# Sixteen modulation tiles moved from the second output layer to the last down layer of a two-block transformer kernel

## What is computed

```python
def second_block(x, c, w_mod, b_mod, ...):
    c_act = jax.nn.silu(c)
    mod = (c_act @ w_mod[l] + b_mod[l])[:, None, :]
    sh_m, sc_m, g_m, sh_f, sc_f, g_f = jnp.split(mod, 6, axis=-1)
    h = rmsnorm(x, mix_pre_w[l]) * (1 + sc_m) + sh_m
    y = hybrid_mixer(h, w_in[l], conv_w[l], ..., w_out[l])
    x = x + g_m * rmsnorm(y, mix_post_w[l])
    h = rmsnorm(x, ffn_pre_w[l]) * (1 + sc_f) + sh_f
    y = conv_ffn(h, w_up[l], ffn_conv_w[l], w_down[l])
    x = x + g_f * rmsnorm(y, ffn_post_w[l])
    return x
```

## Time and profile before

| | us |
|---|---|
| runs, median of 3 | 2451.34 (2451.24 to 2452.98) |
| the profiled execution's own time | 2453.18 |
| its span in the profile | 2451.3 |
| PE busy | 2429.1 (99%) |
| DVE busy | 1781.8 (73%) |
| ACT busy | 1158.0 (47%) |
| POOL busy | 124.0 (5%) |

### The profile page before, as it was taken

The page is one execution under the profiler, slowest core; times in us unless marked ns, Lnnn a source line. Parts: engine busy times, 40 slices in busy tenths (PEclk is TensorE's granted clock), DMA queues, the critical chain, the costliest instruction groups (busy, mean ns, idle before and its releaser), DMA issues.

```text
span 2451.3 us, 35393 instructions
## 1 busy us (share of the span) xinstructions
PE 2429.1 (99%) x13044; PEld 2096.0 (86%) x13044; DVE 1781.8 (73%) x2380; ACT 1158.0 (47%) x1292; POOL 124.0 (5%) x230
## 2 busy tenths in 40 slices
PE   9999999999999999999999999999999999999998
PEld 8888888888888888888888888887888888888887
DVE  5778777699898898677656677777776777775444
ACT  6454445444444444444445445455544444444443
POOL 0000000001000000011002000000000000000000
PEclk9999999999999999999999999999999999999999
DMA  7778775688888888899864655576666666666665
GB/s 256 248 251 264 224 232 187 196 271 288 280 275 293 279 280 276 265 310 309 279 193 143 183 167 163 174 248 217 196 187 185 191 188 187 186 190 199 194 194 166
DMA packets 261233, 552.27 MB, mean 225 GB/s; under 512 B 17256, under 2 KB 18592, under 8 KB 261008
## 3 DMA queue, kind: packets, MB, share of 16 engines
q1 hardware_dynamic: 229344, 442.55, 56.9%
q0 software_dynamic: 28096, 102.82, 13.3%
q10 hardware_dynamic: 3696, 5.56, 0.8%
HBM read 548.73 MB, written 2.14 MB: 225 GB/s over the span
## 4 chain that ended last, share of the span: by engine, by line
PE 92%; DVE 4%; DMA 2%; ACT 1%; issue 1%; SPq 0%; DVEq 0%; POOLq 0%; ACTq 0%
PE PS L1841 36%; PE PS L1848 19%; PE PS L1812 11%; PE PS L1813 11%; PE PS L1814 11%; DMA mod_w<-in_w_mod_rows 1%; DVE w_lo L1107 1%; DVE mod_w L1087 1%; PE PS L1834 1%; PE PS L2168 1%; DMA xr<-in_x 0%; ACT w_hi L579 0%; PE PS L1906 0%; PE PS L1917 0%; DMA w_raw<-in_w_out 0%
## 5 line engine op out<-in xcount | busy, mean ns | idle before, releaser
L579 ACT ACTIVATE w_hi<-w_raw 128x1024 fp32r<-128x1024 f32 x832 | 879.9, 1059 | 1103.6 <-PE PS L1848 589.4
L1107 DVE TENSOR_TENSOR w_lo<-w_raw,w_hi 128x1024 fp32r<-128x1024 f32 x832 | 1015.0, 1225 | 504.5 <-ACT w_hi L579 490.7
L1841 PE MATMUL PS<-xs,w_hi 128*128 128x512 f32 x4024 | 1000.5, 393 | 0.0
L1841 PEld LDWEIGHTS PS<-xs,w_hi 128*128 128x128 f32 x4024 | 727.9, 189 | 133.3 <-issue 0.3
L1848 PEld LDWEIGHTS PS<-xs,w_lo 128*128 128x128 f32 x4096 | 550.0, 191 | 34.5
L1848 PE MATMUL PS<-xs,w_lo 128*128 128x256 f32 x4096 | 561.9, 283 | 0.0
L1812 PE MATMUL PS<-w_hi,hs 128*128 128x512 f32 x704 | 274.4, 390 | 0.0
L1813 PE MATMUL PS<-w_lo,hs 128*128 128x512 f32 x704 | 274.1, 389 | 0.0
L1814 PE MATMUL PS<-w_hi,hs 128*128 128x512 f32 x704 | 274.1, 389 | 0.0
L1087 DVE SCALAR_TENSOR_TENSOR mod_w<-mod_w,c_row 128x1024 f32<-128x1024 f32 x192 | 234.3, 1220 | 26.8 <-DMA mod_w<-in_w_mod_rows 26.7
L1812 PE MATMUL PS<-w_hi,xs 128*128 128x512 f32 x448 | 178.0, 397 | 7.1 <-DVE w_lo L1107 4.9
(11 more groups left out here) (297 smaller groups left out, 1377.4 us busy)
## 6 DMA issues: line engine op xcount, KB each, us to landing
w_raw<-in_w_up SPq DMA_DIRECT2D x352, 512.0 KB, 4.5
w_raw<-in_w_in SPq DMA_DIRECT2D x208, 512.0 KB, 4.3
mod_w<-in_w_mod_rows POOLq DMA_DIRECT2D x192, 512.0 KB, 6.3
w_raw<-in_w_down SPq DMA_DIRECT2D x176, 512.0 KB, 4.7
w_raw<-in_w_out SPq DMA_DIRECT2D x64, 512.0 KB, 4.4
w_raw<-in_w_ple_gate SPq DMA_DIRECT2D x32, 512.0 KB, 4.6
xr<-in_x SPq DMA_DIRECT2D x4, 512.0 KB, 8.7
w_raw<-in_w_ple_proj SPq DMA_DIRECT2D x4, 512.0 KB, 4.6
```

The costliest lines, as they stand in the source:

```text
L579: nc.scalar.activation(w_hi[:, slot, :, :], w_raw[:, slot, :, :], ACT.Copy).then_inc(hi_made, 1)
L1107: V.tensor_tensor(w_lo[:, slot, :, :], w_raw[:, slot, :, :], w_hi[:, slot, :, :].bitcast(F32), ALU.subtract).then_inc(lo_made, 1)
L1841: ins = M(PS[:, bank + b, :], w_hi[:, slot, k, b * P:(b + 1) * P], x(cs[k]), start=begin and k == 0, stop=end and k == GK - 1)
```

## The change

The last 16 tiles leave `out2` and go into the first strip of `down2`, at groups 6 to 18 (13 groups; 16 tiles, so three groups have two). POOL waits for `up2`'s end before it loads them. Summing the vector moves to step (0, 19) of `down2`, turning it on PE to (0, 20), its store to (0, 20), and the first gain row's load from (0, 14) to (0, 20), right behind the store. The other strips load their rows at j = 14 as before.

```diff
@@ class Layer
-        at, groups = j - first, self.G - first
-        if at < 0:
+        at, groups = j - first, self.mod_end - first
+        if not 0 <= at < groups:
             return ()
@@ plan_layers
-        "out2": Layer(2, g16, unrolled=True, mod=176, mods=(6, 6, 4), rows="all", late=True, lead=4),
+        "out2": Layer(2, g16, unrolled=True, rows="all", late=True, lead=4),
         "up2": Layer(11, g16),
-        "down2": Layer(2, g44, unrolled=True, rows="all", lead=4),
+        "down2": Layer(2, g44, unrolled=True, mod=176, mods=(16,), mod_first=(6,), mod_end=19, rows="all", lead=4),
@@ gpsimd
-            with pool.Fori(0, layers["out2"].mod // MOD_HALVES) as block:
+            with pool.Fori(0, layers["down2"].mod // MOD_HALVES) as block:
                 mod_load(block)
...
-            with pool.Fori(layers["out2"].mod // MOD_HALVES, MOD_TILES // MOD_HALVES) as block:
+            pool.wait_ge(evac_done, 2 + layers["up2"].end)
+            with pool.Fori(layers["down2"].mod // MOD_HALVES, MOD_TILES // MOD_HALVES) as block:
                 mod_load(block)
@@ scalar
             def down2_beside(n, j):
                 down2_side(n, j)
-                if (n, j) == (0, 10):
+                if (n, j) == (0, 20):
                     store_gain("down2", 0, 1)
-                if j == layers["down2"].G - 8:
+                if (n, j) == (0, 20) or n and j == layers["down2"].G - 8:
                     load_gain("down2", n, 1)
@@ vector
-            def out2_side(n, j):
-                if (n, j) == (3, 1):
-                    mods_read(MOD_TILES)
-                    add_parts(5 * KC, 6 * KC)
-                    V.tensor_tensor(gate_f, gate_f, pcols("ffn_post_w_2"), ALU.mult).then_inc(S["gate_vec_made"], 1)
-
-            stream("out2", to_post(POST2, z1, "mixed", OUTER), side=out2_side)
+            stream("out2", to_post(POST2, z1, "mixed", OUTER))
...
-            stream("down2", to_post(POSTF, z2, "res_made", OUTER_LAST), side=down2_side)
+            def down2_beside(n, j):
+                down2_side(n, j)
+                if (n, j) == (0, 19):
+                    mods_read(MOD_TILES)
+                    add_parts(5 * KC, 6 * KC)
+                    V.tensor_tensor(gate_f, gate_f, pcols("ffn_post_w_2"), ALU.mult).then_inc(S["gate_vec_made"], 1)
+
+            stream("down2", to_post(POSTF, z2, "res_made", OUTER_LAST), side=down2_beside)
@@ tensor
             def down2_side(n, j):
                 after_up("up2", n, j)
-                if (n, j) == (0, 9):
+                if (n, j) == (0, 20):
                     pe.wait_ge(evac_done, 2 + layers["up2"].end)
                     turn_gain("down2", 0, gate_f)
```

More of the change, by code:

```diff
@@ L55, with __init__ @@
     count_h = 0
-    def __init__(self, pairs, groups, unrolled=False, mod=None, mods=(), mod_first=(), rows=(), late=False, lead=0):
+    def __init__(self, pairs, groups, unrolled=False, mod=None, mods=(), mod_first=(), mod_end=None, rows=(), late=False, lead=0):
         self.pairs, self.G, self.unrolled, self.late, self.lead = pairs, groups, unrolled, late, lead
         self.rows = range(2 * pairs) if rows == "all" else rows
-        self.mod, self.mods, self.mod_first = mod, mods, mod_first
+        self.mod, self.mods, self.mod_first, self.mod_end = mod, mods, mod_first, mod_end or groups
         self.g0, self.n0, self.h0 = Layer.count_g, Layer.count_n, Layer.count_h
```

## The result

The changed kernel takes 2473.35 us (median of 4 runs, 2472.03 to 2474.9), the kernel before 2452.0 us in the same comparison (2451.24 to 2452.98). The ratio is 1.0091 (95% interval 1.0079 to 1.0103): **slower by 21 us**, against 22.3 us forecast.

A forecast was written before the change was run, and what follows sets the result against it. It took PE to bound the kernel, and transfers of tiles and weights together the middle of `out2`. Its terms, -5.3 + 25.9 + 1.7 = +22.3 us, gave a median of 2474 us, range 2462 to 2485.

The forecast's parts named there:

- `out2`'s holes: In `out2`'s second and third strips, PE's lost time goes when the tiles leave: minus 5.3 us.
- vector late at PE: In `down2`, PE waits for the vector before its transpose and starts group 21 late: plus 25.9 us.
- clock behind it: In `down2` behind the vector, one stretch of nine matmuls runs at the low clock: plus 1.7 us.
- gain row: In `down2` after the transpose, store and load back to back cost nothing, covered by a margin of 0 to 2 us.
- The interval of the tiles: In `down2`'s first strip, the last fourteen tiles come every 3.6 us, taken between 3.3 of DMA time and 4.16.
- The lower bound of 3.3 "of DMA time": In `down2`, one tile with its weights takes 3.06 us of all engines, 3.3 us at the 0.92 share.
- The first landing: In `down2`, the first tile's load is issued at 2225.1 and lands 6.3 us later, at 2231.4.
- The first (hidden, faster): Rival: the tiles fit into `down2`'s free room and only the 5.3 us count, 2446 us; 3 in 100.
- the second (quick tiles): Rival: in `down2` tiles land in little over 3 us, 2.6 us each, net +3.5, 2455 us; 5 in 100.
- The estimate of 3.2 us: For one 512 KB tile load, the skill's fit: about 2.0 us plus bytes at 436 GB/s; the sum does not use it.
- The third (holes stay): Rival: `out2` keeps its holes because they come from its weight loads, +27.6, 2479 us; 3 in 100.
- The fourth (low clock for long): Rival: in `down2` groups 21 to 24 all run at 1.2 GHz, 9.6 us for 1.7, 2481 us; 5 in 100.

The follow-up runs named there:

- no_tiles_early: Changed kernel without the 16 tiles, vector at (0, 4), transpose (0, 9), store (0, 10), load j = 14: 2448.16 us against 2450.16 for the kernel before.
- no_tiles_late: Changed kernel without the 16 tiles, its late vector, transpose, store and load kept: 2449.70 us against 2450.16 for the kernel before.
- spread_front: Kernel before with its 16 tiles spread over `out2`'s strips as 5, 5, 4, 2, vector made at (0, 6) of `down2`: 2447.68 us against 2450.81.
- ring4: Changed kernel with the 16 tiles of `down2` going through four slots in place of two: 2457.90 us against 2450.49 for the kernel before.
- dose8: Changed kernel with eight tiles kept in `out2` (4 and 4) and eight in `down2`: 2449.83 us against 2450.8 for the kernel before.
- vector_early: Changed kernel with its tiles, but the vector made before them at (0, 4) and an early chain: 2466.77 us against 2450.16 for the kernel before.
- filler_short: Changed kernel with 40 matmuls on constants on PE ahead of its wait for the vector: 2471.69 us against 2450.8 for the kernel before.

## Why the prediction was right, point by point

**Direction and size.** Forecast +22.3 us (2474, range 2462 to 2485), measured +21.35 and 2473.35. The terms, against the trace after:

| term | forecast | measured |
|---|---|---|
| `out2`'s holes | -5.3 | -5.3 (3.8 in a second trace; 2.0 by the times of `no_tiles_early`) |
| vector late at PE | +25.9 | +24.5 |
| clock behind it | +1.7 | +2.7 |
| gain row | 0 | 0 (nor in `no_tiles_late`) |
| sum | +22.3 | +21.9 (22.0 between the spans) |

The sum is nearer than its terms: the vector came 1.4 us sooner than forecast, and the clock cost 1.0 us more. That these two nearly cancel is luck.

**`out2`'s holes** came from the tiles: gone in all runs without six tiles in a strip. The step that was too simple is its size: I took one execution's 5.3 us as the kernel's. I had noted that this execution lay 1.8 us above the median, and left the term as it was. The prediction's reading that the transfers as such bound the middle of `out2` was too wide, too. The second strip asks for six tiles in 21.8 us, one every 3.6, and from the first tile to the twelfth they came every 4.1 (1619.75 to 1664.81), about what two slots give by the prediction's own 4.14. DVE falls behind by that, until PE's lead is used up and the largest hole opens. The twelfth tile in the kernel before, with `w_lo` behind it, just ahead of PE's matmul at 1667.24:

```profile
1664.81 1.23 DVE L1087 SCALAR_TENSOR_TENSOR mod_w<-mod_w,c_row 128x1024 f32<-128x1024 f32 x1 [2.62 <-DMA mod_w<-in_w_mod_rows]
```

`spread_front` asks every 4.35 us at the same bytes per second and has no hole, which fits; four slots in `out2` were not tried, so for `out2` the slots are argued and not shown.

**The interval of the tiles.** 3.6 us was taken for the fourteen behind the second tile, a choice between two bounds, and 3.42 measured (3.34 over all fifteen). The mechanism, the round of two slots, is confirmed by `ring4`. The sign that the prediction gave, a tile every 3.3 to 4.2 us, holds for the mean and not for each. The lower bound of 3.3 "of DMA time" was not a bound, though it lay close to the result: `ring4` had tiles every 2.35 us. What was right is that the tiles land sooner where weights are asked for less often: 4.7 us where the earlier trace rows have 6.3, and 6.7 in `dose8`, whose weights are hardly held back. The first landing was taken at 6.3 and was longer: from its issue at 2220.29, with the other slot's beside it, to the tile's start at 2227.58 are 7.3 us. That made the second tile 1.4 us later than in the working and the fourteen intervals made the end 2.5 us earlier, so the vector came 1.1 us sooner, counted from `down2`'s start, and PE with the shorter hand-over 1.4.

**The wait for the vector.** Group 21 stood 10.7 us behind it, and `vector_early` prices what it adds to the tiles at 9.1 us. The prediction's sentence that the lead is worth nothing at this wait holds.

**The clock.** Nine matmuls were forecast, as after the hole in `out2`; all twelve of group 21 were slow, so +2.7 in place of +1.7. `filler_short` shows that it is the clock. That the low clock inside the zone (0.84 and 0.85) cost nothing there, as was said, fits a PE that waits at its end anyway; no run shows it by itself.

**The gain row** came in time, with more room than the 0 to 2 us forecast: DVE stood 6.0 us for it, and the weights behind it were ready 4.3 us before PE took them up.

**The rivals.** The first (hidden, faster) and the second (quick tiles) fell: no tile of the zone landed in under 4.2 us, and already eight tiles, in `dose8`, cost PE 3.5 us more than none. The estimate of 3.2 us for such a transfer, from the Trainium skill ("DMA: Bandwidth & Descriptors", section "Anatomy of one DMA — SWDGE (gpsimd) path"), was not met by any of the 192 loads of the changed kernel, 4.1 us at best; here each shares the engines with the weights. The third (holes stay) is refuted by every trace without the tiles. The DMA share was forecast near 0.9 up to the last tile; it is 0.84 and 1.03 in the zone, and 0.59 in the 10.7 us in which PE stands. The fourth (low clock for long) was half true: it lasted a group, not four.

## What to carry to other kernels

Work that streams through a small ring has a shortest interval, (issue to landing, plus the time from use to the next issue) over the number of slots. Compare it with the interval at which the new place asks, before moving the work, and spread the work until the place asks more seldom. Take the landing time from a stretch where the other streams run at full rate: 6.3 us and 4.1 per tile here. The 4.7 us and 3.3 per tile of the change were seen only where the tiles held the weights back. Put nothing that waits for the stream's end on the bottleneck engine with ready work behind it: that wait added 9 of 27 us here. The same 16 tiles over four strips, clear of the layer's last evacuation, gave `out2` without holes and 3.1 us, without the move.

## What the runs showed that I had not expected

The page's share of DMA time is no fixed price per load. It gave 1.67 and 1.70 us for 512 KB at 16 engines; in `ring4` the engines moved 402 GB/s at a share of 1.04, which is 1.36 us for the same load (512 KB at 402 GB/s are 1.30 us, times the share). The strips of the kernel before at 0.92 and 0.93, 316 and 310 GB/s, were below what the engines moved there. And the same share of 0.93 and the same 316 GB/s went with holes in one kernel and without any in `spread_front`, where a tile was asked for every 4.35 us in place of 3.6 and the vector was made later: the share alone does not tell whether transfers starve an engine.
